# Two residual blocks with three expert mixtures: a new order of experts with 32-row steps, and another home for clearing and modulation

## The chip, the cores and the metric

The kernel is one program on one core of a Trainium2 chip, in fp32. The metric is the device time of one execution in microseconds (us). Its five engines are PE (matmul), DVE and ACT (elementwise), POOL (GpSimd; here also indirect DMA) and SP, which issues most DMA.

## The reference, cut to what matters

The input x has 512 tokens of 1024 values; the second block also has a context of 256 tokens.

```python
def first_block(...):     # x: 512 x 1024
    h = rms_norm(x, norm_mix)                  # one linear for three branches
    # RWKV branch + differential attention (subln on its heads), gated, w_out
    x = x + mixer(h)
    x = x + hierarchical_moe(rms_norm(x, norm_ffn), ...)          # f1
    x = x + gate(rms_norm(x, norm_ple) @ w_ple_gate) * (p @ w_ple_proj)

def second_block(...):
    for l in range(2):
        mod   = silu(c)     @ ada_w[l] + ada_b[l]    # 6 rows of 1024
        mod_c = silu(c_ctx) @ ada_w[l] + ada_b[l]
        # even (l = 0): attention + pooling; odd (l = 1): neighbourhood attention
        x = x + g1 * mixer(modulate(rmsnorm(x), sh1, sc1))
        x = x + g2 * hier_moe(modulate(rmsnorm(x), sh2, sc2))     # f2, f3
    return rmsnorm(x, final_g)

def hier_moe(h, ...):     # f2: 768 tokens (with the context), f3 and f1: 512
    # best of 4 groups, then the 2 best of its 8 experts per token
    yb = (silu(xb @ w1[e]) * (xb @ w3[e])) @ w2[e]     # 32 experts, 1024 -> 512 -> 1024
    return scatter_add(weights * yb)
```

## The kernel before

The phases follow one another, each in its own block on all engines: `n1` norm, `rp` features, `rr` `rwkv_prepare`, `rc` `rwkv_chunks`, `rs` scan, `rf` `rwkv_finish`, `l1` linear, `h1` heads, `a1` `difference_phase`, `sub` `subln_phase`, `ty` and `to` transposes, `l3`, `tm`, `l5`; the mixture f1 (`f1r` routing, `f1e` experts); `np` norm, `pq`, `lg` linear; `ne` norm, `le`, `he`, `ae`, `lf`; f2; `no` norm, `lo`, `lv`, `ao`, `lr`; f3; `nf` norm. A phase begins when all engines have ended the one before.

**Experts.** `experts_phase` (L2301) takes 32 steps, one expert each. Every expert has 6 pieces of weights of 1 MB, which SP streams into a ring of SBUF slots of that size (19 in f1, 18 in f2 and f3): the first ones (`FIRST`: 17, 14, 15) are asked for at the start of routing, the other 2, 4 and 3 slots exist only in the experts phase (`grow`, L2271), and each later piece waits until PE has used the piece in its slot (`used`). In f2 and f3 the first three experts are fixed (29, 30, 31), so that their weights can be loaded before the routing is known; the others are ranked by load in the routing. `Plan` (L85) gives each step its width: 64 rows, 128 in the wide steps (6, 10, 18, 22, 26 in f2; 9, 19, 24 in f3), and a huge one (14) of two columns of 128 and 64 rows with the same weights. The n_wide most loaded ranks go to huge and wide steps, the rest in order of load to the others. f1 takes its experts in their own order at 64 rows. Tokens beyond a step's rows go to overflow passes of 128 rows (up to `MAXOV` = 19), written out behind the steps and run only if there are any. POOL gathers each step's token rows from `hbuf` (L2285) and scatters its results to `ybuf` (L2374). In a step of 64 rows PE puts the two halves of the output columns on partitions 0 to 63 and 64 to 127, DVE evicts y in one copy from 128 partitions (L2568), and the scatter sends 128 half rows of 2 KB. `Combine` later gathers each token's two rows from `ybuf`, weighs and adds them in the following norm phase (`np`, `no`, `nf`).

**Routing.** `route_phase` (L1811) norms the tokens, loads the router weights with two strided DMAs straight into `wr` (L1888, L1889: packets of 4 and of 32 values), then biases and table, and behind them the first weight pieces (L2279), all on SP.

**Modulation.** `mod` is computed beside other phases by `ModulationSide` in groups (layer, third): 8 pieces of 1 MB each, 4 matmuls of 2 rows per piece (L2802), a bias matmul (L2806), two strips of 512 columns copied by ACT (L2782) and two scaled by DVE, or all four by ACT, then a store to `modD`. `begin` loads a ring of pieces, the biases and the gain rows; `rest` loads the others as slots come free; `finish` stores. PE's first matmul waits for biases and gains together. `steps` tells how many pieces PE takes between the turns of a norm or heads phase. Homes: (0,0) and (0,1) in l1 and h1, (0,2) in np, (1,0) in ne, (1,1) in he and ae, (1,2) in no.

**Clearing.** `Clear` (L2812 on) zeroes a tile in `rr` and writes it over `ybuf`, 13 blocks of 2 MB, and a padded bias table (`relpad`), all from SP in `rc` (L2835, L2838); `clear.end` waits in l1.

## Time and profile before

| | us |
|---|---|
| median of 3 runs (lowest, highest) | 3363.59 (3363.01, 3367.09) |
| the profiled execution | 3371.78 |
| its span (mean granted clock 0.907) | 3370.0 |
| PE busy | 2734.9 (81%) |
| DVE busy | 1038.0 (31%) |
| ACT busy | 735.1 (22%) |
| POOL busy | 398.2 (12%) |
| HBM read, written | 784.29 MB, 67.08 MB |

The busy shares are means over stages of different kinds. The three mixtures lie at about 724 to 1260 (f1), 1762 to 2331 (f2) and 2795 to 3332 (f3); the rest is norms, linears, attention and the RWKV scan. A row of a window view reads: stretch, its length, busy us of PE, PE's weight loads, DVE, ACT and POOL with their numbers of instructions, the clock granted to PE as a share of 2.4 GHz, the mean busy share of the 16 DMA engines, and what they moved in GB/s. A timeline row reads: start, duration, engine, line, operation, tiles, and in brackets the idle time before it with what ended it.

### The profile page before, as it was taken

The numbers are of one execution on the slowest core, as the hardware profiler recorded it, in microseconds if no ns is written. First come the engines' busy times: TensorE is split into PE (matmuls) and PEld (weight loads), VectorE is DVE, ScalarE is ACT, GpSimd is POOL, SyncE is SP. The second block draws the span as 40 slices with busy tenths as digits, with TensorE's granted clock in tenths as the row PEclk, the third lists the DMA queues.
The fourth block names the chain that finished last, engine by engine and source line by source line (L and its number), as shares of the span: only waits on it lengthen the run. The fifth ranks groups of instructions, "written<-read, shape, count | busy, mean of one in ns | idle before, by whom it ended". The sixth has DMA issues, their size and how long they took to land. (4 is left out here: it accounts for less than half of the span.)

```text
span 3370.0 us, 42335 instructions
## 1 busy us (share of the span) xinstructions
PE 2734.9 (81%) x16276; PEld 1612.7 (48%) x16276; DVE 1038.0 (31%) x2048; ACT 735.1 (22%) x1436; POOL 398.2 (12%) x510
## 2 busy tenths in 40 slices
PE   7866896779888875695976999995788985999994
PEld 5666772663333323483763433442576773333331
DVE  3524317541111113426535111112612644111113
ACT  3412234221000003213612000001311752000001
POOL 0122000001111111000100111112000510111111
PEclk9889998889999996897997999998799997999998
DMA  4090523159999986422028999998401128999996
GB/s 132 7 338 22 166 60 152 60 186 406 410 407 410 414 342 213 153 79 103 5 75 348 402 406 416 413 414 339 157 13 55 30 62 308 401 415 414 417 420 246
DMA packets 217304, 826.99 MB, mean 245 GB/s; under 512 B 59279, under 2 KB 84111, under 8 KB 137228
## 3 DMA queue, kind: packets, MB, share of 16 engines
q1 hardware_dynamic: 189868, 747.55, 56.9%
q0 software_dynamic: 27232, 76.68, 6.2%
q8 instruction: 134, 2.20, 0.3%
q14 instruction: 70, 0.57, 0.0%
HBM read 784.29 MB, written 67.08 MB: 253 GB/s over the span
## 5 line engine op out<-in xcount | busy, mean ns | idle before, releaser
L2430 PE MATMUL f1e_psum_up<-f_raw,f1e_xT 128*64 128x512 f32 x712 | 208.5, 648 | 46.9 <-DMA f_raw<-in_w_up_dram 39.1
L2430 PE MATMUL f3e_psum_up<-f_raw,f3e_xT 128*64 128x512 f32 x640 | 157.6, 615 | 13.6 <-DMA f_raw<-in_moe_w_dram 13.6
L254 PE MATMUL l_psum_acc<-l_w_hi,m_hT_hi 128*128 128x512 f32 x288 | 114.8, 399 | 30.4 <-DVE l_w_lo L248 30.4
L2430 PEld LDWEIGHTS f1e_psum_up<-f_raw,f1e_xT 128*64 128x64 f32 x712 | 60.3, 147 | 139.0 <-issue 136.3
L256 PE MATMUL l_psum_acc<-l_w_hi,m_hT_lo 128*128 128x512 f32 x288 | 113.9, 396 | 0.0
L255 PE MATMUL l_psum_acc<-l_w_lo,m_hT_hi 128*128 128x512 f32 x288 | 113.3, 393 | 0.0
L2285 POOL DMA_INDIRECT f_xin<-hbuf,g_src x98 | 94.1, 960 | 119.0 <-DVE g_src L2170 72.0
L2430 PE MATMUL f2e_psum_up<-f_raw,f2e_xT 128*64 128x512 f32 x432 | 101.0, 600 | 6.4 <-DMA f_raw<-in_moe_w_dram 6.4
L2519 ACT ACTIVATE f2e_xT<-f2e_psum_xT 128x512 f32<-128x512 f32 (+1 forms) x33 | 22.3, 675 | 363.8 <-PE f2e_psum_xT L2398 363.8
L2519 ACT ACTIVATE f3e_xT<-f3e_psum_xT 128x512 f32<-128x512 f32 (+1 forms) x33 | 21.4, 649 | 332.9 <-PE f3e_psum_xT L2398 332.9
L2430 PEld LDWEIGHTS f3e_psum_up<-f_raw,f3e_xT 128*64 128x64 f32 x640 | 45.9, 140 | 87.3 <-issue 84.9
L2577 DVE TENSOR_TENSOR f1e_h<-f1e_sig,f1e_psum_up 64x512 f32<-64x512 f32 x32 | 21.7, 679 | 210.1 <-ACT f1e_sig L2530 210.1
L2519 ACT ACTIVATE f1e_xT<-f1e_psum_xT 128x512 f32<-128x512 f32 x32 | 19.1, 597 | 307.3 <-PE f1e_psum_xT L2398 307.3
L248 DVE TENSOR_TENSOR l_w_lo<-l_raw,l_w_hi 128x512 fp32r<-128x512 f32 x70 | 48.2, 692 | 123.1 <-ACT l_w_hi L243 123.0
L254 PE MATMUL lo_psum_acc<-o_hT_hi,lo_w_hi 128*128 128x512 f32 (+1 forms) x192 | 71.5, 373 | 16.9 <-DVE lo_w_lo L248 8.8
L2374 POOL DMA_INDIRECT ybuf<-f1e_y,g_dst x32 | 32.5, 1015 | 426.7 <-PE f1e_psum_xT L2398 386.1
L2450 PE MATMUL f1e_psum_y<-f_raw,f1e_hT 128*64 128x512 f32 x344 | 80.7, 604 | 1.9 <-DMA f_raw<-in_w_down_dram 1.0
L2577 DVE TENSOR_TENSOR f3e_h<-f3e_sig,f3e_psum_up 64x512 f32<-64x512 f32 (+1 forms) x33 | 22.5, 681 | 190.2 <-ACT f3e_sig L2530 160.4
L2577 DVE TENSOR_TENSOR f2e_h<-f2e_sig,f2e_psum_up 64x512 f32<-64x512 f32 (+1 forms) x33 | 22.5, 681 | 188.2 <-ACT f2e_sig L2530 143.5
L2568 DVE COPY f2e_y<-f2e_psum_y 128x512 f32<-128x512 f32 (+1 forms) x33 | 26.0, 789 | 173.7 <-PE f2e_psum_y L2450 173.7
L2568 DVE COPY f3e_y<-f3e_psum_y 128x512 f32<-128x512 f32 (+1 forms) x33 | 25.0, 756 | 169.7 <-PE f3e_psum_y L2450 169.7
L254 PEld LDWEIGHTS l_psum_acc<-l_w_hi,m_hT_hi 128*128 128x128 f32 x288 | 55.0, 191 | 41.9 <-DVE l_w_lo L248 30.8
(884 smaller groups left out, 6058.1 us busy)
## 6 DMA issues: line engine op xcount, KB each, us to landing
f_raw<-in_moe_w_dram SPq DMA_DIRECT2D x209, 1024.0 KB, 27.9
c_y<-in_moe_w_dram SPq DMA_DIRECT2D x64, 1024.0 KB, 27.7
f_raw<-in_w_gate_dram SPq DMA_DIRECT2D x45, 1024.0 KB, 28.8
f_raw<-in_w_up_dram SPq DMA_DIRECT2D x44, 1024.0 KB, 29.3
f_raw<-in_w_down_dram SPq DMA_DIRECT2D x43, 1024.0 KB, 29.5
c_rows<-in_moe_w_dram SPq DMA_DIRECT2D x41, 1024.0 KB, 28.4
...
```

Of the source, the lines that this page charges most:

```text
L248: return v.tensor_tensor(dst, src, hi.bitcast(F32), ALU.subtract)
L254: pe.matmul(out, lh, rh, start=first, stop=False)
L255: pe.matmul(out, lh, rl, start=False, stop=False)
L256: return pe.matmul(out, ll, rh, start=False, stop=last)
L2285: pool.indirect_dma_start(out=self.xin[q % 2][0:rows, :], out_offset=None, in_=hbuf[0:n * P, :], in_offset=bass.IndirectOffsetOnAxis(ap=R. ...
L2374: pool.indirect_dma_start(out=yh, out_offset=place, in_=y[q % 2][:, 0:512], in_offset=None, bounds_check=2 * N * P - 1, oob_is_err=False). ...
L2430: mm = pe.matmul(out[lo:lo + HALF, :], x[:, kk * HALF:(kk + 1) * HALF], w[z][:, k * FF:(k + 1) * FF], start=(kk == 0), stop=(kk == KD - 1))
L2450: mm = pe.matmul(out, lhs, w[:, c:c + 512], start=(kk == 0), stop=(kk == KF - 1))
L2519: act.activation(xT[q % 2][:, 0:cols], px[:, 0:cols], ACT.Copy).then_inc(x_out, 1)
L2568: v.tensor_copy(y[q % 2][:, 0:cols], py[:, 0:cols]).then_inc(y_done, 1)
L2577: v.tensor_tensor(h[0:rows, :], sg[0:rows, :], pu[banks_of[q][-1]][0:rows, :], ALU.mult).then_inc(h_done, 1)
```

## The change

- `Plan` gets `slim_at`: steps of 32 rows (3 to 10 in f2, 3 to 14 in f3) for the least loaded ranks, right behind the three fixed experts. Wide steps move to 13, 17, 21, 25, 28 (huge 15) in f2 and to 17, 21, 25 (huge 19) in f3. In a slim step PE works on four strips of 32 columns: gate and up each as two strips of 256 output columns, y as four strips of 256.
- Each step scatters whole rows of `ybuf` from its own 32, 64 or 128 partitions; the eviction of y is split, DVE taking the lower 512 columns (`y_low`), ACT the upper (`y_high`). `MAXOV` goes from 19 to 23 and the blocks to clear from 13 to 14.
- The whole ring exists from the start of routing: the slots that were made late are lent to the routing for rows and tokens, and their pieces are asked for as the routing gives them back. The router weights come contiguous into `wgc` and `wec`, and POOL copies them into `wr`. PE's and DVE's waits for weights and biases part.
- Clearing: 6 blocks in `rr`, 3 in `rf`, 5 and `relpad` in `a1`; `clear.end` in l3.
- Modulation: (0,2) moves from np to `a1` (first 4 pieces) and `sub`; the first pieces of (1,0) are loaded in lg, the rest from POOL in ne, with a ring of 2 that (1,1) then takes over; the spacing changes in ne, he and no; gain rows are waited for by DVE alone, biases just ahead of their matmul.

```diff
-MAXOV = 19
+MAXOV = 23
 SLOTS = (NE + 1 + MAXOV) * P
 HALF = P // 2
+QUART = P // 4
...
+        self.slim_from = NE - len(fixed) - len(slim_at)
         self.n_pass = NE + 1 if self.sorted else NE
-        self.width = [P if s in wide_at or s == huge_at else HALF for s in range(NE)] + [HALF]
+        self.width = [P if s in wide_at or s == huge_at else QUART if s in slim_at else HALF for s in range(NE)] + [HALF]
...
+            elif step in self.slim_at:
+                out.append(slim)
+                slim += 1
...
-RANKED = {NTA: Plan(FIXED, (6, 10, 18, 22, 26), 14), NT: Plan(FIXED, (9, 19, 24), 14)}
+RANKED = {NTA: Plan(FIXED, (13, 17, 21, 25, 28), 15, (3, 4, 5, 6, 7, 8, 9, 10)),
+          NT: Plan(FIXED, (17, 21, 25), 19, (3, 4, 5, 6, 7, 8, 9, 10, 11, 12, 13, 14))}
...
-        if mix:
+        if mix or side and not whole:
             @block.gpsimd
             def _(pool):
-                mix.pool(pool)
+                if mix:
+                    mix.pool(pool)
+                if side and not whole:
+                    side.rest(pool)
...
+            clear.write(sp, 0, 6)
...
-            clear.write(sp)
...
+            clear.write(sp, 6, 9)
...
+        halves = [[h[:, i * D:(i + 1) * D] for i in range(2)] for h in stream.lend()]
+        tok = [h[:, :] for h in stream.xin] + halves.pop(0)
+        rows_home = [h for pair in halves for h in pair]
+        many = sum(1 if k[1] is None else 2 for k in kinds)
+        rows_home += [s.sb(f"row{i}", [P, D])[:, :] for i in range(len(rows_home), many)]
+        SC, SH = [], []
+        for k in kinds:
+            SC.append(rows_home.pop(0))
+            SH.append(rows_home.pop(0) if k[1] is not None else None)
+        own_hT = [h.rearrange("p (k t) -> p k t", t=P) for h in rows_home[:2]]
+        hT = own_hT + [s.sb(f"hT{i}", [P, KD, P])[:, :, :] for i in range(len(own_hT), 2)]
...
+            sp.dma_start(wgc[:, :, :], wg.rearrange("(p k) n -> p k n", p=P)).then_inc(wr_in, 16)
+            sp.dma_start(wec[:, :, :], we.rearrange("(p k) n -> p k n", p=P)).then_inc(wr_in, 16)
             sp.wait_ge(padded, 2)
-            sp.dma_start(wr[:, :, 0:NG], wg.rearrange("(p k) n -> p k n", p=P)).then_inc(wr_in, 16)
-            sp.dma_start(wr[:, :, 8:NL], we.rearrange("(p k) n -> p k n", p=P)).then_inc(wr_in, 16)
-            sp.dma_start(br[:, 0:NG], bc_row(bg, NG)).then_inc(wr_in, 16)
-            sp.dma_start(br[:, 8:NL], bc_row(be, NE)).then_inc(wr_in, 16)
+            sp.dma_start(br[:, 0:NG], bc_row(bg, NG)).then_inc(br_in, 16)
+            sp.dma_start(br[:, 8:NL], bc_row(be, NE)).then_inc(br_in, 16)
...
-            stream.first(sp)
+            stream.first(sp, 0, stream.n_first)
+
+            for t in range(2, min(n, TOKS)):
+                sp.wait_ge(stored[t], 16)
+                sp.wait_ge(t_done, 2 * t + 2)
+            stream.first(sp, stream.n_first, stream.n_first + 1)
+            sp.wait_ge(h_done, n)
+            sp.wait_ge(lt_done, n)
+            stream.first(sp, stream.n_first + 1, stream.ring)
 
         @block.gpsimd
         def _(pool):
+            pool.wait_ge(wr_in, 32)
+            pool.tensor_copy(wr[:, :, 0:NG], wgc[:, :, :]).then_inc(wr_done, 1)
+            pool.tensor_copy(wr[:, :, 8:NL], wec[:, :, :]).then_inc(wr_done, 1)
...
-                pool.wait_ge(y_done, q + 1)
-                column = plan.order[q][1]
-                place = bass.IndirectOffsetOnAxis(ap=R.dst[:, column:column + 1], axis=0)
-                if wide[q]:
-                    pool.indirect_dma_start(out=ybuf, out_offset=place, in_=y[q % 2][:, :], in_offset=None,
-                                            bounds_check=N * P - 1, oob_is_err=False).then_inc(y_out[q % 2], 16)
-                else:
-                    pool.indirect_dma_start(out=yh, out_offset=place, in_=y[q % 2][:, 0:512], in_offset=None,
-                                            bounds_check=2 * N * P - 1, oob_is_err=False).then_inc(y_out[q % 2], 16)
+                pool.wait_ge(y_low, q + 1)
+                pool.wait_ge(y_high, q + 1)
+                column, rows = plan.order[q][1], rows_of[q]
+                pool.indirect_dma_start(out=ybuf, out_offset=bass.IndirectOffsetOnAxis(ap=R.dst[0:rows, column:column + 1], axis=0),
+                                        in_=y[q % 2][0:rows, :], in_offset=None, bounds_check=N * P - 1, oob_is_err=False
+                                        ).then_inc(y_out[q % 2], 16)
...
+                if slim[q]:
+                    for k in range(KF):
+                        for b in range(2):
+                            r = slice(QUART * b, QUART * b + QUART)
+                            part = h[r, 0:FF // 2].rearrange("t (p k) -> t k p", k=KF)[:, k, :]
+                            mm = pe.matmul(ph[HALF * b:HALF * b + HALF, k * QUART:(k + 1) * QUART], part,
+                                           tab[r, C_IDENT + QUART * b:C_IDENT + QUART * b + QUART], start=True, stop=True)
+                    mm.then_inc(ht_done, 1)
+                    return
...
+                elif slim[q]:
+                    w = [stream.have(pe, q, 2 * half + z) for z in range(2)]
+                    out = pu[banks_of[q][0]]
+                    for k in ks:
+                        kk = 4 * half + k
+                        for z in range(2):
+                            for b in range(2):
+                                lo = HALF * (1 - z) + QUART * b
+                                c = k * FF + FF // 2 * b
+                                mm = pe.matmul(out[lo:lo + QUART, 0:FF // 2], x[:, kk * QUART:(kk + 1) * QUART], w[z][:, c:c + FF // 2],
+                                               start=(kk == 0), stop=(kk == KD - 1))
+                            if k == 3:
+                                mm.then_inc(used, 1)
...
+                        for g in range(4 if slim[q] else 0):
+                            c = k * D + D // 4 * g
+                            mm = pe.matmul(py[QUART * g:QUART * g + QUART, 0:D // 4], hT[:, kk * QUART:(kk + 1) * QUART],
+                                           w[:, c:c + D // 4], start=(kk == 0), stop=(kk == KF - 1))
...
+            def take_y(q):
+
+                act.wait_ge(used, stream.index[q, 5])
+                if q >= 2:
+                    act.wait_ge(y_out[q % 2], 16 * (q // 2))
+                if slim[q]:
+                    act.activation(y[q % 2][0:QUART, 512:768], py[2 * QUART:3 * QUART, 0:256], ACT.Copy)
+                    act.activation(y[q % 2][0:QUART, 768:D], py[3 * QUART:P, 0:256], ACT.Copy).then_inc(y_high, 1)
+                elif wide[q]:
+                    act.activation(y[q % 2][:, 512:D], py[:, 512:D], ACT.Copy).then_inc(y_high, 1)
+                else:
+                    act.activation(y[q % 2][0:HALF, 512:D], py[HALF:P, 0:512], ACT.Copy).then_inc(y_high, 1)
...
-                cols = D if wide[q] else D // 2
-                v.tensor_copy(y[q % 2][:, 0:cols], py[:, 0:cols]).then_inc(y_done, 1)
+                if slim[q]:
+                    v.tensor_copy(y[q % 2][0:QUART, 0:256], py[0:QUART, 0:256])
+                    v.tensor_copy(y[q % 2][0:QUART, 256:512], py[QUART:2 * QUART, 0:256]).then_inc(y_low, 1)
+                else:
+                    rows = rows_of[q]
+                    v.tensor_copy(y[q % 2][0:rows, 0:512], py[0:rows, 0:512]).then_inc(y_low, 1)
...
+            v.wait_ge(self.g_in, 16 * sum(len(x) for x in self.scaled))
...
-            pe.wait_ge(self.b_in, 64 * len(self.groups) + 16 * sum(len(x) for x in self.scaled))
...
+                pe.wait_ge(self.b_in, 64 * len(self.groups))
...
+            side.rest(sp)
...
+            side.scalar(act, 0)
...
+        third = modulation.side(m, [(0, 2)], 4, lent=True)
...
+            def between(sp):
+                side.finish(sp)
+                third.begin(sp)
+                clear.write(sp, 9, clear.blocks)
...
-        side = modulation.side(m, [(0, 2)], 3)
-
-        def fetches(sp):
-            early(sp)
-            side.begin(sp)
-        norm_phase(nc, "np", xs, tab, A["norm_ple"], hT=hT, ahead=fetches, mix=mix, side=side, steps=(2, 2, 2, 2))
+        norm_phase(nc, "np", xs, tab, A["norm_ple"], hT=hT, ahead=early, mix=mix)
+        home = Scope(nc, "nm", keep=True, side="right")
+        side = modulation.side(home, [(1, 0)], 2)
...
-            side = modulation.side(r, [(1, 0)], 3)
-
-            def fetches(sp):
-                side.begin(sp)
-                ahead.fetch(sp)
             norm_phase(nc, "ne", xs, tab, A["norm_mix_g_2"][0], hT=hT, mods=[mods[is_x(t)] for t in range(NTA)],
-                       ahead=fetches, side=side, steps=(1, 2, 2, 1, 1, 1))
+                       ahead=ahead.fetch, side=side, steps=(2, 2, 2, 1, 1))
...
-                       side=modulation.side(w, [(1, 2)], 3), steps=(2, 3, 3), whole=True)
+                       side=modulation.side(w, [(1, 2)], 3), steps=(0, 2, 2, 2, 1, 1), whole=True)
```

## Rows read from the trace of the kernel before

**Rows 1.** Page, part 2: DMA share and GB/s in 40 slices

```profile
...
DMA  4090523159999986422028999998401128999996
GB/s 132 7 338 22 166 60 152 60 186 406 410 407 410 414 342 213 153 79 103 5 75 348 402 406 416 413 414 339 157 13 55 30 62 308 401 415 414 417 420 246
...
```

**Rows 2.** Windows of the f2 stage: busy us per engine, granted clock, DMA share, GB/s

```profile
...
core 0: us, PE busy (x) PEld busy (x) DVE busy (x) ACT busy (x) POOL busy (x), PEclk, DMA share, GB/s
1800.00:1820.00 20.00, 7.52 (x31) 6.76 (x32) 14.85 (x65) 0.32 (x2) 0.00 (x0) 0.51 0.84 353
1820.00:1840.00 20.00, 11.75 (x50) 5.03 (x52) 6.17 (x26) 2.48 (x3) 2.89 (x3) 0.64 0.63 237
1880.00:1900.00 20.00, 20.00 (x101) 7.81 (x98) 2.49 (x4) 2.21 (x3) 3.21 (x4) 1.00 1.02 404
...
2280.00:2300.00 20.00, 15.36 (x68) 6.01 (x68) 2.10 (x4) 1.19 (x2) 1.97 (x2) 0.91 1.01 401
...
```

**Rows 3.** Windows of the f3 stage

```profile
...
2880.00:2900.00 20.00, 20.00 (x98) 7.54 (x96) 2.90 (x5) 1.78 (x3) 2.87 (x3) 1.00 1.02 388
3060.00:3080.00 20.00, 20.00 (x82) 8.35 (x82) 3.02 (x4) 1.19 (x2) 1.96 (x2) 1.00 1.01 423
3280.00:3300.00 20.00, 16.53 (x80) 6.72 (x82) 2.90 (x5) 1.72 (x3) 1.97 (x2) 1.00 1.02 425
...
```

**Rows 4.** Timeline of DVE: the h product of two half steps and the one behind a wide

```profile
...
1889.99 0.68 DVE L2577 TENSOR_TENSOR f2e_h<-f2e_sig,f2e_psum_up 64x512 f32<-64x512 f32 x1 [4.52 <-ACT f2e_sig L2530]
...
1902.30 0.68 DVE L2577 TENSOR_TENSOR f2e_h<-f2e_sig,f2e_psum_up 64x512 f32<-64x512 f32 x1 [4.59 <-ACT f2e_sig L2530]
...
1938.34 0.68 DVE L2577 TENSOR_TENSOR f2e_h<-f2e_sig,f2e_psum_up 64x512 f32<-64x512 f32 x1 [4.00 <-ACT f2e_sig L2530]
...
```

**Rows 5.** Timeline of SP: f2's first issues in the experts phase

```profile
...
1827.93 2.26 SPq L2346 DMA_DIRECT2D f2e_raw<-in_moe_w_dram  x4
1836.71 0.36 SPq L2346 DMA_DIRECT2D c_rows<-in_moe_w_dram  x1
...
```

**Rows 6.** Timeline of SP: the issue behind the router loads, f1 and f3

```profile
...
725.82 1.76 SPq L1890 DMA_DIRECT2D f1r_br<-in_b_group_dram  x1
...
2797.23 3.14 SPq L1890 DMA_DIRECT2D f3r_br<-in_moe_b_group_dram  x1
...
```

**Rows 7.** Window of f1, all steps of 64 rows

```profile
...
1000.00:1020.00 20.00, 17.10 (x74) 6.30 (x72) 1.79 (x3) 1.19 (x2) 1.96 (x2) 0.91 1.01 414
...
```

**Rows 8.** Waits in np and in ne: us in total, times, longest

```profile
...
PE np_psum_ada L2802 <- DMA pl_adag<-in_norm_ffn_g_dram: 33.0, 1, 33.0
ACT pl_hT_hi L243 <- PE np_psum_pt L430: 21.9, 5, 13.5
...
PE ne_psum_ada L2802 <- DMA e_adag<-in_norm_mix_g_dram: 25.5, 1, 25.5
...
```

**Rows 9.** Timeline of np, DVE: start, us, line, tiles

```profile
...
1285.28 1.28 DVE L2684 SCALAR_TENSOR_TENSOR np_first<-c_y,g_f1wts,np_first 128x1024 f32<-128x1024 f32 x1 [2.06 <-DMA c_y<-ybuf,g_f1slots]
...
1297.99 0.69 DVE L248 TENSOR_TENSOR pl_hT_lo<-np_psum_pt,pl_hT_hi 128x512 fp32r<-128x512 f32 x1 [8.71 <-ACT pl_hT_hi L243]
...
1316.25 1.29 DVE L248 TENSOR_TENSOR pl_hT_lo<-np_psum_pt,pl_hT_hi 128x512 fp32r<-128x512 f32 x2 [0.46 <-ACT pl_hT_hi L243]
...
```

**Rows 10.** Windows of rr (113), rf (319) and subln (596)

```profile
...
113.00:162.00 49.00, 35.18 (x168) 25.30 (x172) 36.10 (x47) 30.11 (x52) 16.81 (x12) 0.72 0.00 0
319.00:337.00 18.00, 0.00 (x0) 0.00 (x0) 16.88 (x30) 5.67 (x9) 0.00 (x0) 0.59 0.03 7
596.00:606.00 10.00, 0.00 (x0) 0.00 (x0) 9.43 (x7) 1.07 (x2) 0.00 (x0) 0.50 0.05 7
...
```

**Rows 11.** Window in which the clears are written now

```profile
...
180.00:250.00 70.00, 46.13 (x1268) 44.65 (x1268) 15.86 (x14) 10.15 (x17) 21.85 (x18) 0.89 1.03 377
...
```

**Rows 12.** Timeline of PE in np: the last pieces of the side

```profile
...
1309.75 1.89 PE L2802 MATMUL np_psum_ada<-pl_adaw,g_silu_c 128*2 128x512 f32 x8
...
1313.29 1.04 PE L2806 MATMUL np_psum_ada<-pl_adab,g_tab 1*2 1x512 f32 x8
...
```

More of the change, by code:

```diff
@@ L100, in ranks @@
     def ranks(self):
-        large, small, last = 1, self.n_wide, NE - len(self.fixed)
+        large, small, slim, last = 1, self.n_wide, self.slim_from, NE - len(self.fixed)
         out = list(range(last, NE))
@@ L327, in _ @@
                 ahead(sp)
-            if side:
-                if whole:
-                    side.begin(sp)
+            if side and whole:
+                side.begin(sp)
                 side.rest(sp)
-                if whole:
-                    side.finish(sp)
+                side.finish(sp)
             if out is not None:
@@ L2239, in __init__ @@
         self.row_slots, self.lent = by_end[:len(onward.row_tiles)], by_end[:len(lent)]
-        own = iter([s.sb(f"raw{i}", [P, self.COLS]) for i in range(first - len(lent))])
-        self.raw = [lent[self.lent.index(slot)] if slot in self.lent else next(own) for slot in range(first)]
-        self.raw_in = [s.sem(f"raw{i}") for i in range(first)]
+        own = iter([s.sb(f"raw{i}", [P, self.COLS]) for i in range(self.ring - len(lent))])
+        self.raw = [lent[self.lent.index(slot)] if slot in self.lent else next(own) for slot in range(self.ring)]
+        self.raw_in = [s.sem(f"raw{i}") for i in range(self.ring)]
         self.spare = [slot for slot in range(first) if slot not in self.lent][:self.PER]
@@ L2269, in __init__, with lend, first @@
         self.place = {piece: q for q, piece in enumerate(self.fetched)}
-    def grow(self, s):
-        more = range(self.n_first, self.ring)
-        self.raw += [s.sb(f"raw{i}", [P, self.COLS]) for i in more]
-        self.raw_in += [s.sem(f"raw{i}") for i in more]
-    def first(self, sp):
-        for q, (step, j) in enumerate(self.fetched[:self.n_first]):
+    def lend(self):
+        return [self.raw[slot] for slot in range(self.n_first, self.ring)]
+    def first(self, sp, a, b):
+        for q in range(a, b):
+            step, j = self.fetched[q]
             sp.dma_start(self.raw[q][:, :], self.src[j][self.plan.fixed[step]]).then_inc(self.raw_in[q], 16)
@@ L2308, in experts_phase @@
     N = plan.n_pass
-    wide = [plan.width[column] == P for step, column in plan.order]
+    rows_of = [plan.width[column] for step, column in plan.order]
+    wide = [rows == P for rows in rows_of]
+    slim = [rows == QUART for rows in rows_of]
     UP = 3
@@ L2336, in _ @@
         def _(sp):
-            for q in range(stream.n_first, len(stream.fetched)):
+            for q in range(stream.ring, len(stream.fetched)):
                 step, j = stream.fetched[q]
-                if q >= stream.ring:
-                    sp.wait_ge(used, stream.freed(q - stream.ring))
+                sp.wait_ge(used, stream.freed(q - stream.ring))
                 if step < len(plan.fixed):
@@ L3023, in first_mixer @@
                 linear(lhs, KD, allt, win[:, 3328:5376], 2048, gate_evac, on="a")],
-                early=side, late=clear.end)
+                early=side)
             qT, kT = q.sb("qT", [P, 4, SEQ]), q.sb("kT", [P, 4, SEQ])
@@ L3091, in ple @@
                                 linear(operand(pT), 2, allt, A["w_ple_proj"], D, add, behind=0)], ahead=ahead,
-                     late=side.finish)
+                     early=side)
+    return home, side
 def gated_add(rows_of, xs, G):
@@ L3129, in even_mixer @@
         pj = m.sb("pj", [P, NTA, 1280])
-        under = modulation.side(m, [(1, 1)], 2)
+        under = modulation.side(m, [(1, 1)], 2, lent=True)
+        under.W = side.W
         with Scope(nc, "e3") as r:
@@ L3302, in fused_blocks @@
         if stage("ple"):
-            ple(nc, tab, A, xq, modulation, behind)
+            home, side = ple(nc, tab, A, xq, modulation, behind)
         ctx = g.sb("ctx", [P, XT0, D])
```

176 lines of the change are left out of this document (95 added, 81 removed).

## The prediction

> **What bounds the kernel now.** I read the page's slices first [rows 1]. Three stretches of the span have the DMA share at 9 with 400 to 420 GB/s: the three mixtures of experts (f1, f2, f3), over half of the time. Elsewhere DMA is mostly idle and PE, or a chain of ACT and DVE, sets the pace. Then the windows by 20 us inside f2 and f3 [rows 2, 3]: share 1.00 to 1.02 from the start of the experts to a few us before their end, while PE has idle time in the last ones (15.36 of 20 at 2280, 16.53 at 3280). So the experts end when their last weight piece lands; 192 pieces of 1.05 MB have to come whatever the order of the experts. What moves an end there is bytes, bytes per second, or the moment the stream starts and stops. Last I read the phases around the moved modulation and clearing, by waits and timelines: np, subln, ne, the router heads.
>
> **The order of the experts: 0 in the middle, +1 at the end of f3.** PE's period is 12.25 us for a 64-row step (1889.99 to 1902.30) and 23.8 for a 128-row one (1902.30 to 1938.34 is one wide and one half) [rows 4]. The stream needs longer than a half step: 6 pieces are 6.29 MB, with the token rows about 6.7 MB, and at 408 GB/s 16.4 us. A 32-row step has no row; its ends are well under half of 12.25 and all of it. I take 7 us, nearest to a half step with its columns side by side, and it does not matter: anything below 16.4 waits for weights. What a slim step saves is idle time of PE. What the order does change is how far PE lags when the wide steps come late. In f3, from lag 0 at step 17: +7.6, −4, +20 (the expert run over two columns, taken as about 36 us), −4, +7.6, −12, +7.6, and six half steps at −4 each end near 0; the peak is 27 us. With 18 pieces of 2.6 us the ring holds 47, so the stream should go on, though with few requests in flight. For f2 the same sum peaks near 24 and ends at 0. I take +1 for f3, bounds 0 to +8 over both.
>
> **More pieces before the routing ends: 0.** In f2 DMA has 14 pieces done before the experts begin (share 0.84, then 0.63 in the next window) [rows 2], and 4 more are asked for at 1827.93, the first one into a freed slot at 1836.71 [rows 5]. After the change the 4 come early, in idle time, but the next must still wait for the first freed slot near 1837: 4 pieces (10 us) less to carry, 9 to 10 us of fresh idleness. Net −1 to +2.6; I take 0. In f1 and f3 DMA runs on from the first piece, so the order of issue buys nothing; the new waits on SP (stored tokens, h_done, lt_done) have only these pieces behind them.
>
> **Router weights: −2 in f1, −3 in f3, 0 in f2.** The 16-byte and 128-byte packets of the two router loads hold SP: the issue behind them takes 1.76 us in f1 and 3.14 in f3 [rows 6], where a plain issue takes 0.36 [rows 5]. Contiguous loads bring the first weight piece forward by 1.4 and 2.8, with a little for the cheaper issues themselves, one for one where DMA then never stops. f2 has slack before its experts. Two POOL copies and three small DVE operations of 0.15 to 0.2 us each in the order of ranks, with 23 rows for 19, lengthen routing by 0.3 to 0.6, which is +0.5 in f2. Bounds for the whole: −6 to +1.
>
> **Scatter of whole rows: 0, with a large upper bound.** A 64-row step used to send y from 128 partitions in halves; now 64 (or 32) partitions send whole rows of 4 KB. Bytes are equal. The gather already goes to 64 partitions in those steps, and there the stream is slower: 388 GB/s at 2880 with half steps of many tokens, against 423 at 3060 around a wide step and 425 at 3280 with small experts [rows 3]; f1, all in half steps, runs at 414 [rows 7]. 388 for 423 over 20 us is 1.6 us for some 100 gathered rows. The gathers alone explain it, if writing into few partitions crowds the weights, which are written too; the scatter reads. I take 0, as reads and writes are the nearest difference, and keep 16 us per thousand rows as the upper end. The eviction of y, now half on DVE and half on ACT, was one DVE copy of 0.69; its place behind the last weights stays about as long, and ACT's wait for y_out has slack: 0 ± 0.3 per stage.
> The Trainium skill, "SBUF — State Buffer", section "Door 1: The DMA port swizzle", says that partitions 0 to 63 reach only 8 of the 16 ports, and 0 to 31 the same 8. That agrees with the slower windows beside gathers; it does not say whether reads and writes meet at a port. By it alone the scatter would now be confined as the gather is, and the sum would be the third rival's.
>
> **Modulation (0,2) leaves np: −21.** In np PE waits 33.0 us for the gain rows that the side's first matmul wants, and ACT 21.9 for PE's transposes [rows 8]. DVE is idle for 8.71 us up to 1297.99, that is from 1289.3 on; its last operation is at 1316.25 to 1317.54 [rows 9]. Without the side the last combine (its data used at 1285.28) sets the end: it, the add, the square and the norm, each about 1.28 as that row (1285.3 to 1290.5), two turns on PE near 1.0 each, the high halves on ACT and the low ones on DVE at 0.69 each, and on DVE the backlog of earlier tiles at 1.4 each. That chain ends at 1295 to 1297. 1317.5 − 1296.3 = 21.2. Bounds −15 (the gathers, in POOL's queue, land no earlier and turns pile up) to −24 (they no longer share DMA with 3 MB).
>
> **It enters subln: +11.** Today 10.3 us of DVE alone, PE at 0 and clock 0.50 [rows 10]. Four of 8 pieces come in the difference phase behind nothing, but 5 clearing blocks are issued behind them: 4.2 + 10.5 MB at 377 GB/s [rows 11] are 39 us, the relpad rows some 9 more, from 551 to about 600. PE takes 1.9 us per piece at that clock [rows 12], frees the slots at 598 to 604, and the other four land 5 to 8 us after that, behind the rest of the clearing: 606 to 613. Then 1.9 for the last, 1.04 for the bias [rows 12], and about 1.4 each for ACT and DVE to take two strips of 512 columns each (at 0.69 each) [rows 9]: 617 against 606. Bounds +8 to +15. The difference phase ends with SP's last issue near 595, just where it ends now: +1 (0 to +3). finish in ty: +0.5.
>
> **Clearing in rr and rf: +1.** Six blocks of 2.1 MB (34 us) fall in 113 to 162, where DMA stands at 0.00, and three in 319 to 337 at 0.03 [rows 10]; the last lands near 338 to 341, just ahead of l1's first weights. rc gives up its writing, for which nothing waited.
>
> **(1,0) leaves ne's front, (1,1) and (1,2) re-spaced: −1.** In ne PE waits 25.5 us for the gain [rows 8] and ends the phase with side work; with two pieces in SBUF beforehand and the gain waited for only by DVE, it ends 2 us earlier (−5 to +2: a ring of 2 costs a landing per pair; POOL, which issues the rest, has nothing else there). In no, DVE paces: +1 (0 to +2). lg and he: 0, their PE works on loads that stay within 2 to 4 tenths of DMA [rows 1] and cover 2 to 4 MB more.
>
> **Sum.** −21 + 11 + 1 + 0.5 + 1 − 1 = −8.5; experts 1 + 0 − 5 + 0.5 = −3.5; together −12 of the profiled execution's 3371.8, of which 3370.0 is span: 3359.8. That execution is 8.2 above the median of the runs, 3363.6; carried over, 3351.6. I shade it to 3353 because edits costed at 0 seldom come below it.
>
> **Rivals.**
> 1. The stream gains too: PE catches up early, slots come free sooner, and the early windows of f2 and f3, now 404 and 388 [rows 2, 3], come up to f1's 414 or part of the way, 2 to 4% over 150 us each. For it: those windows have PE at 20.00. Against: DMA share is 1.01 there already. It would give 5 to 10 more: 3345.
> 2. np gives half (its turns and combine stay late) and subln costs +15, or the late wide steps run the ring dry for some us: −12 + 6 + 4 + 4, 3366, no change.
> 3. Slower: the scatter from 64 partitions crowds the weights as the gather does. 1024 rows of f1, about 1000 in f2's and 650 in f3's steps below 128, at 16 us per thousand, are 43 us at most; reads of the scatter may overlap half, so +15 to +43. It decides from 12 us on. At the middle, 3353 + 30: 3383. For it: only steps below 128 rows show slow windows. Against: that the windows show one direction's collision already paid.
> 4. The change doesn't do what it says: an expert overflows its 32 rows and passes over again. By the sorted loads of these inputs, from the reference, the slim ranks hold at most 29 tokens, so I give it next to nothing.
>
> **Chances.** Forecast 0.45, rival 1 0.12, rival 2 0.2, rival 3 0.21, rest 0.02. About 0.2% (6.7 us) is what a measurement of this kernel tells from no change: 3356.9 to 3370.3. The forecast's own range is 3346 to 3361, some of it inside that band. Faster 0.58, same 0.2, slower 0.22. The range for 8 in 10 runs from 3343 to 3386, to the middle of rival 3.
>
> **What would show it.** After: np without a side ends some 36 us after f1's last y, not 57; subln lasts 21 us with PE in it; first f1 piece issued 1.7 us after today's distance from the phase start; f2's DMA idle until its first freed slot; in f2 and f3 the h products of slim steps spaced 16 us, not 7. If windows of half steps in f1 fall below their 414 GB/s [rows 7] while the DMA share stays at 1.0, rival 3 is right; if they rise, rival 1. The forecast is wrong if the expert stages move by more than 5 us in all, or np and subln together by other than −10 ± 5.

## The result, and the profile after

The changed kernel took 3329.86 us in the median of 4 runs (3326.91 to 3337.80), the kernel before 3365.34 (4 runs, 3363.01 to 3377.89) on that occasion: ratio 0.9891, 95% interval 0.9861 to 0.9921. Measured a second time beside other kernels it was 3330.61 (ratio 0.9891, 0.9875 to 0.9908). The gain is about 36 us where I forecast 10, and the time lies below my range (3343). The direction was right; about three quarters of the gain came from a place to which I gave the price 0.

The profiled execution took 3337.80 us with a span of 3336.0, against 3371.78 and 3370.0. This table takes the length of a stage as the time from the last instruction of the stage before it to its own last one, in each kernel's profiled execution. "Clears moved" is the kernel before with that part of the change alone; the last column is the second profile of the changed kernel. The stages that are left out differ by 2 us at most.

| stage | before | clears moved | after | after, again |
|---|---|---|---|---|
| rr | 46.7 | 45.2 | 43.4 | 45.2 |
| rc (rwkv_chunks) | 114.2 | 87.9 | 87.4 | 87.9 |
| rs | 44.2 | 44.3 | 46.3 | 43.8 |
| l1, h1, a1 | 258.1 | 257.7 | 262.0 | 257.7 |
| sub | 10.6 | 10.6 | 22.9 | 21.3 |
| l5 | 47.9 | 49.1 | 49.0 | 49.1 |
| f1r + f1e | 541.0 | 540.4 | 538.2 | 537.6 |
| np | 53.8 | 52.5 | 33.3 | 33.2 |
| pq, lg | 66.0 | 65.7 | 66.2 | 65.0 |
| ne | 48.0 | 47.7 | 44.3 | 44.6 |
| f2r + f2e | 574.7 | 572.1 | 573.7 | 573.1 |
| f3r + f3e + nf | 572.1 | 574.7 | 572.9 | 571.8 |

What differs between the last two columns (rs, a1's group, rr) is what one profiled execution differs from another. What differs from the first in both is rc, sub, np, ne and f1.

**rc.** The windows of both kernels at the same times, inside rwkv_chunks: before, with the clears in it,

```profile
...
180.00:200.00 20.00, 13.64 (x405) 13.17 (x403) 4.88 (x4) 2.99 (x5) 6.82 (x6) 0.94 1.03 379
200.00:220.00 20.00, 13.38 (x382) 13.00 (x382) 3.82 (x4) 2.39 (x4) 4.99 (x4) 0.91 1.04 383
220.00:240.00 20.00, 12.46 (x344) 11.96 (x346) 5.18 (x6) 3.58 (x6) 7.49 (x6) 0.91 1.03 381
...
```

and after, without:

```profile
...
180.00:200.00 20.00, 18.40 (x617) 18.08 (x615) 7.32 (x6) 4.08 (x8) 8.74 (x8) 1.00 0.02 4
200.00:220.00 20.00, 16.10 (x485) 15.59 (x482) 7.26 (x7) 3.82 (x7) 8.49 (x7) 0.91 0.01 3
220.00:240.00 20.00, 18.41 (x617) 18.08 (x614) 7.37 (x7) 3.58 (x6) 7.62 (x6) 1.00 0.02 4
...
```

DMA share 1.03 to 1.04 against 0.01 to 0.02, and PE gets through 344 to 405 matmuls in 20 us against 485 to 617. The waits of the kernel before over this stage (engine, line, waited for: us in total, times, longest) name no DMA tile and no other engine for the difference, but "issue", which is idle time in which the engine waited for nothing that the profile shows:

```profile
...
PE ri_psum_p L1551 <- issue: 11.5, 4, 3.3
PE ri_psum_p L1560 <- issue: 10.2, 5, 3.6
...
PE ri_psum_p L1564 <- issue: 1.1, 1, 1.1
...
```

The first two lines are 21.7 us in 9 stops, all three 22.8 us in 10 stops of up to 3.6 us. After, the same view has no such line for a PE matmul; DVE's wait for PE (63.0 us before) is

```profile
...
DVE ri_x L1609 <- PE ri_psum_p L1571: 40.3, 16, 7.9
...
```

Behind "issue" stand PE's own instructions. The page counts instructions as DMA queues of their own; the one below has packets of 16 KB (2.20 MB in 134):

```profile
...
q8 instruction: 134, 2.20, 0.3%
...
```

In the records of that queue, before, the packets in this stage start at 184.7, 191.7, 198.9, 206.2, 213.5, 220.5 us and so on; after, at 182.8, 187.2, 191.3, 195.4, 199.8, 4.1 to 4.4 apart where PE runs through and 4.6 in the mean of the stage. The stage issues 2176 matmuls of 64 columns and as many weight loads and takes 17 of these packets, 256 such instructions for each, so that PE eats a packet in some 4 us; with busy DMA engines the next one came after 7.3 in the mean.

That this queue feeds PE shows in the stops: each of the 10 before ends 1.3 to 1.5 us after a packet of it has landed (the packet of 191.7 lands at 192.6, and PE goes on at 194.1; that of 206.2 at 207.2, and PE goes on at 208.7). Over the five kernels with traffic in rc, all 45 stops on "issue" end 1.2 to 1.6 us after a landing; the changed kernel and the one with the clears moved have none. A packet takes 0.9 to 1.4 us on its way with and without traffic, so it starts late; since when it was asked for, the trace doesn't say.

Not all of the difference is idle time. In the kernel with the clears moved rc is 26.3 us shorter: PE is idle for 21.1 us less (35.6 to 14.5) and busy for 5.2 us less (78.6 to 73.4) with the same 2176 matmuls. The granted clock hardly differs over the stage (0.89 before, 0.90).

**np and the issue order** went as forecast, **sub** by its length. In np no modulation is left; PE waits for DVE's norm, and DVE for the gathers:

```profile
...
PE np_psum_pt L435 <- DVE np_h L410: 28.3, 4, 22.7
...
DVE np_first L2759 <- DMA c_y<-ybuf,g_f1slots: 11.5, 3, 8.2
...
```

In sub PE takes the four pieces that were there, then waits 4.46 us for the fifth:

```profile
...
571.87 5.45 PE L2877 MATMUL sub_psum_ada<-m_adaw,g_silu_c 128*2 128x512 f32 x32 [0.71 <-PEq L207]
581.79 1.29 PE L2877 MATMUL sub_psum_ada<-m_adaw,g_silu_c 128*2 128x512 f32 x8 [4.46 <-DMA m_adaw<-in_ada_w_dram]
584.28 1.89 PE L2877 MATMUL sub_psum_ada<-m_adaw,g_silu_c 128*2 128x512 f32 x8 [1.20 <-DMA m_adaw<-in_ada_w_dram]
...
591.03 1.88 PE L2882 MATMUL sub_psum_ada<-m_adab,g_tab 1*2 1x512 f32 x8
...
```

SP shows when the missing pieces are asked for. It is held by the clears and relpad up to 570.1, and the refetches, whose turn comes in sub and behind its gain row, are issued at 574.86:

```profile
...
533.57 22.84 SPq L2912 DMA_DIRECT2D ybuf<-m_zeros  x5
556.45 13.66 SPq L2917 DMA_DIRECT2D relpad<-m_relrows  x2
...
574.86 3.50 SPq L2825 DMA_DIRECT2D m_adaw<-in_ada_w_dram  x4
...
```

The clears are the smaller part of that: with none of them in a1 (the last experiment) the refetches go out 2.0 us behind the gain row's issue instead of 3.0 and land in 7.6 us in the median instead of 9.0, but sub is still 19.9 us.

The issues that stood behind the strided router loads [rows 6] take 0.43 us now, in f1,

```profile
...
715.39 0.43 SPq L1906 DMA_DIRECT2D f1r_br<-in_b_group_dram  x1
...
716.81 0.43 SPq L2310 DMA_DIRECT2D f_raw<-in_w_gate_dram  x1
...
```

and in f3:

```profile
...
2761.97 0.43 SPq L1906 DMA_DIRECT2D f3r_br<-in_moe_b_group_dram  x1
...
2763.60 0.43 SPq L2310 DMA_DIRECT2D c_y<-in_moe_w_dram  x1
...
```

From the phase's first issue (714.07 in f1, 2760.18 in f3) to the first weight piece it is 2.7 us in f1 for 4.5 before, and 3.4 in f3 for 6.3.

**The experts.** Windows after; they answer to [rows 2, 3, 7]:

```profile
...
1000.00:1020.00 20.00, 16.73 (x76) 6.29 (x76) 2.47 (x5) 2.38 (x4) 1.85 (x2) 0.91 1.02 415
1200.00:1220.00 20.00, 18.25 (x83) 7.16 (x80) 2.47 (x4) 2.38 (x4) 1.86 (x2) 0.91 1.02 422
1784.00:1804.00 20.00, 11.31 (x50) 4.79 (x52) 5.19 (x20) 2.51 (x4) 2.82 (x3) 0.66 0.47 162
1840.00:1860.00 20.00, 17.11 (x267) 11.15 (x268) 3.59 (x10) 3.04 (x8) 3.61 (x4) 1.00 1.01 398
2845.00:2865.00 20.00, 17.70 (x189) 8.45 (x189) 3.32 (x7) 3.09 (x7) 3.69 (x4) 1.00 1.01 409
...
```

f1 runs at 415 and 422 GB/s with its scatter from 64 partitions, no slower than the 414 of before; DMA stands at 0.47 around the end of f2's routing, as predicted. The h products of the 32-row steps in f2 are 8.9 to 9.0 us apart while PE catches up and 16.8 once it has:

```profile
...
1839.82 0.41 DVE L2652 TENSOR_TENSOR f2e_h<-f2e_sig,f2e_psum_up 64x256 f32<-64x256 f32 x1 [4.03 <-ACT f2e_sig L2585]
...
1848.74 0.41 DVE L2652 TENSOR_TENSOR f2e_h<-f2e_sig,f2e_psum_up 64x256 f32<-64x256 f32 x1 [4.07 <-ACT f2e_sig L2585]
...
1866.69 0.41 DVE L2652 TENSOR_TENSOR f2e_h<-f2e_sig,f2e_psum_up 64x256 f32<-64x256 f32 x1 [4.12 <-ACT f2e_sig L2585]
...
1883.51 0.41 DVE L2652 TENSOR_TENSOR f2e_h<-f2e_sig,f2e_psum_up 64x256 f32<-64x256 f32 x1 [3.69 <-ACT f2e_sig L2585]
...
```

### The profile page after: what moved, and what is told of

It reads as the page before. It is cut to its first block and busy times, and to the rows that moved or that the text cites. A ratio compares the mean times of both kernels' runs of the same rounds, so it can differ in the third digit from the quotient of the medians.

```text
span 3336.0 us, 45180 instructions
## 1 busy us (share of the span) xinstructions
PE 2682.3 (80%) x17476; PEld 1626.9 (49%) x17476; DVE 1029.3 (31%) x2072; ACT 788.4 (24%) x1554; POOL 399.3 (12%) x526
## 5 line engine op out<-in xcount | busy, mean ns | idle before, releaser
L2479 PE MATMUL f3e_psum_up<-f_raw,f3e_xT 128*64 128x512 f32 x496 | 131.0, 618 | 13.3 <-DMA f_raw<-in_moe_w_dram 13.3
L2479 PE MATMUL f2e_psum_up<-f_raw,f2e_xT 128*64 128x512 f32 x480 | 114.8, 612 | 8.6 <-DMA f_raw<-in_moe_w_dram 8.6
L2468 PE MATMUL f3e_psum_up<-f_raw,f3e_xT 128*32 128x256 f32 x688 | 64.5, 496 | 31.7 <-DMA f_raw<-in_moe_w_dram 31.5
L2652 DVE TENSOR_TENSOR f1e_h<-f1e_sig,f1e_psum_up 64x512 f32<-64x512 f32 x32 | 21.7, 679 | 210.8 <-ACT f1e_sig L2585 210.8
L2400 POOL DMA_INDIRECT ybuf<-f2e_y,g_dst x33 | 30.7, 931 | 433.1 <-PE f2e_psum_xT L2425 352.8
L2598 ACT ACTIVATE f1e_y<-f1e_psum_y 64x512 f32<-64x512 f32 x32 | 19.0, 594 | 264.1 <-PE f1e_psum_y L2504 264.1
L2400 POOL DMA_INDIRECT ybuf<-f3e_y,g_dst x33 | 30.5, 923 | 420.7 <-PE f3e_psum_xT L2425 352.2
L2652 DVE TENSOR_TENSOR f2e_h<-f2e_sig,f2e_psum_up 64x512 f32<-64x512 f32 (+2 forms) x33 | 20.4, 617 | 188.2 <-ACT f2e_sig L2585 143.5
L2652 DVE TENSOR_TENSOR f3e_h<-f3e_sig,f3e_psum_up 64x512 f32<-64x512 f32 (+2 forms) x33 | 19.3, 584 | 189.7 <-ACT f3e_sig L2585 159.9
L247 ACT ACTIVATE l_w_hi<-l_raw 128x512 fp32r<-128x512 f32 x70 | 44.0, 631 | 122.2 <-PE l_psum_acc L260 108.4
L2455 PE MATMUL f2e_psum_up<-f_raw,f2e_xT 128*128 128x512 f32 x160 | 71.3, 599 | 0.0
```

The lines of the kernel that those rows point to most:

```text
L247: return act.activation(dst, src, ACT.Copy)
L2400: pool.indirect_dma_start(out=ybuf, out_offset=bass.IndirectOffsetOnAxis(ap=R.dst[0:rows, column:column + 1], axis=0), in_=y[q % 2][0:rows ...
L2455: mm = pe.matmul(out[:, :], x[:, kk * P:(kk + 1) * P], w[:, k * FF:(k + 1) * FF], start=(kk == 0), stop=(kk == KD - 1))
L2468: mm = pe.matmul(out[lo:lo + QUART, 0:FF // 2], x[:, kk * QUART:(kk + 1) * QUART], w[z][:, c:c + FF // 2], start=(kk == 0), stop=(kk == KD ...
L2479: mm = pe.matmul(out[lo:lo + HALF, :], x[:, kk * HALF:(kk + 1) * HALF], w[z][:, k * FF:(k + 1) * FF], start=(kk == 0), stop=(kk == KD - 1))
L2652: v.tensor_tensor(h[0:rows, 0:cols], sg[0:rows, 0:cols], pu[banks_of[q][-1]][0:rows, 0:cols], ALU.mult).then_inc(h_done, 1)
```

## The experiments

Each ratio is to the kernel before on the same chip.

### The clears moved, and nothing else

The kernel before with its 13 blocks in rr (6), rf (3) and a1 (4, with relpad).

```diff
+            clear.write(sp, 0, 6)        # rwkv_prepare
...
-            clear.write(sp)              # rwkv_chunks
...
+            clear.write(sp, 6, 9)        # rwkv_finish
...
+                clear.write(sp, 9, clear.blocks)   # a1, behind side.finish
```

> The kernel before with one part of the change: its 13 clearing blocks are written 6 in rr, 3 in rf, 4 and relpad in a1, none beside rwkv_chunks. Theory (the clears' traffic keeps PE waiting for its own instructions: PE shows 21.7 us of 'issue' idle in rc and its 16 KB instruction packets come every 7.2 us instead of 4.1): rc falls from 113 to 87 or 88 us, PE's issue idle there to under 2 us, the whole by 22 to 26 us: 3339 to 3343. Rival (rc is shorter for another reason, the granted clock or where tiles lie in SBUF with the new allocation): rc stays above 105 us and the whole within 5 us of the kernel before.

Measured: 3340.46 us (3340.05 to 3343.51), ratio 0.9914 (0.9893 to 0.9936): some 29 us faster (a little more than expected), rc 87.9. Its windows have the counts of the changed kernel (609, 435 and 617 in the second profile of it), not those of before:

```profile
...
180.00:200.00 20.00, 18.93 (x603) 18.71 (x602) 6.10 (x5) 4.18 (x7) 9.45 (x8) 0.94 0.02 4
200.00:220.00 20.00, 15.85 (x436) 15.50 (x433) 7.30 (x7) 4.18 (x7) 8.24 (x7) 0.83 0.01 3
220.00:240.00 20.00, 18.40 (x617) 18.08 (x613) 7.32 (x6) 4.02 (x7) 8.60 (x8) 1.00 0.02 4
...
```

This part alone gives 29 of the 36 us. The rival, clock or placement, is out: modulation, plan and tiles are those of before, and the granted clock over rc is 0.90 for 0.89.

### The clears back in rwkv_chunks

```diff
+        @block.sync
+        def _(sp):
+            clear.write(sp, 0, clear.blocks)     # rwkv_chunks; none in rr, rf, a1
```

> The kernel after with all 14 blocks and relpad written in rwkv_chunks again. Theory: rc back to 112 to 115 us with 20 us and more of issue idle of PE; sub gets shorter by 1 to 4 us as its last modulation pieces no longer stand behind clears; the whole +20 to +25: 3350 to 3355. Rival (rc's gain has another cause): rc stays near 88 us and the whole falls by the 1 to 4 us of sub.

Measured: 3358.70 us (9 runs, 3348.06 to 3360.89), ratio 0.9969 (0.9958 to 0.9980), 26 us above the changed kernel by the ratios, a little more than expected. The profiled execution is the fastest of the nine, 10.6 us below the median. In it rc is 116.5 us, sub 19.6 instead of 22.9, and PE's stops are back:

```profile
...
PE ri_psum_p L1567 <- issue: 9.3, 5, 3.6
...
PE ri_psum_p L1558 <- issue: 8.8, 4, 3.1
...
```

With 2.0 us on a third line that is 20.1 us in 10 stops. Of rc's 29 us more than in the changed kernel, 18 are idle time of PE; the other 11 are its busy time, 84.0 us for 72.9, at a granted clock of 0.83 over the stage for 0.91.

### One clearing block at a time

```diff
             sp.dma_start(dst, ...).then_inc(self.out, 16)
+            if i < self.blocks - 1:
+                sp.wait_ge(self.out, 16 * (i + 1))
```

> The kernel before, but in rwkv_chunks each clearing block of 2 MB is issued only when the one before has landed, instead of all queued at once (up to four outstanding, 19.2 us from issue to landing). If PE's 16 KB instruction packets wait behind everything that is queued (theory A, depth), one block outstanding lets them through in less: rc falls from 113 us to below 100 and the whole by 12 to 25 us. If they only get a share of busy DMA engines whatever stands behind (theory B, rate), the packets still come every 6.5 to 7.2 us while a block is under way; rc gains less than 8 us, by the gaps of about 2 us between blocks only.

Measured: 3384.22 us (3381.67 to 3388.30), ratio 1.0051 (1.0035 to 1.0068), slower by some 17 us where either theory had it faster. rc fell to 99.0 us, but SP was at the clears and relpad until 284 us, and the next stage waited 25.7 us for its turn. I had not seen that the wait between blocks stretches them past the end of rc. The windows:

```profile
...
180.00:200.00 20.00, 16.79 (x519) 16.47 (x517) 4.88 (x4) 4.23 (x8) 9.15 (x8) 0.93 0.68 250
200.00:220.00 20.00, 15.12 (x449) 14.48 (x446) 8.53 (x8) 2.51 (x5) 5.54 (x6) 0.92 0.62 228
...
```

```profile
...
PE ri_psum_p L1564 <- issue: 6.7, 3, 2.6
...
PE ri_psum_p L1560 <- issue: 2.2, 2, 1.8
...
```

"Issue" is down to 10.1 us in 7 stops. The packets came 3.5 to 8.4 us apart, 5.6 in the mean. Since DMA was busy only 62 to 70% of the time, this separates the two theories badly; hence the next one.

### Two blocks at a time

As above, but block i + 1 waits for block i − 1 (two semaphores in turn).

> The kernel before, with at most two clearing blocks (4 MB) outstanding in rwkv_chunks, so that DMA stays busy (share near 1.0, which one block at a time did not keep: 0.62 to 0.70) while little stands queued. If PE's instruction packets wait behind what is queued (depth), they come every 5.5 to 6.5 us and rc is 97 to 107 us. If the busy share alone sets it (rate), they come every 7 us and more, and rc is 110 us and more as in the kernel before.

Measured: 3367.06 us (10 runs, 3362.58 to 3369.03), ratio 0.9995 (0.9986 to 1.0005), rc 112.6 us.

```profile
...
180.00:200.00 20.00, 15.07 (x406) 14.61 (x404) 4.88 (x4) 2.55 (x5) 5.37 (x5) 0.83 1.03 378
...
220.00:240.00 20.00, 15.67 (x381) 15.40 (x381) 5.91 (x6) 3.58 (x6) 7.53 (x6) 0.74 1.03 378
...
```

```profile
...
PE ri_psum_p L1560 <- issue: 9.4, 4, 3.8
...
PE ri_psum_p L1551 <- issue: 6.8, 4, 3.0
...
```

4 MB outstanding, share 1.03, 18.4 us of "issue" in 9 stops, and the instruction packets are again 7.1 us apart. How much stands queued (19.2 us from issue to landing before, 11.3 here) makes next to no difference, 112.6 us for 114.2; whether the engines are busy all the time does.

### Reads instead of clears in rwkv_chunks

```diff
+            for i in range(28):      # 1 MB each, HBM to a spare tile
+                if i >= 2:
+                    sp.wait_ge(spare_in[i % 2], 16 * (i // 2))
+                sp.dma_start(spare[i % 2][:, :], ...).then_inc(spare_in[i % 2], 16)
+            for z in spare_in:
+                sp.wait_ge(z, 16 * 14)
```

> The kernel after with added traffic in rwkv_chunks: 28 pieces of 1 MB of expert weights read from HBM into two spare tiles, two outstanding, nothing waits for them but the end of the phase. It leaves out nothing. If any busy DMA starves PE of instructions (theory), rc grows from 87 to 105 to 116 us, with issue idle of PE of 10 us and more and instruction packets over 6 us apart: the whole +18 to +29. If it is the writing from SBUF to HBM alone that does it (rival), rc stays below 92 us.

Measured: 3351.01 us (3348.33 to 3354.79), ratio 0.9955 (0.9938 to 0.9971), 21 us above the changed kernel; but only 9.2 us of it is rc (96.6), another 12 is rs, whose start waited 12.2 us for the reads to end. In rc:

```profile
...
180.00:200.00 20.00, 16.71 (x473) 16.23 (x471) 4.88 (x4) 3.95 (x7) 7.91 (x7) 0.88 0.92 358
200.00:220.00 20.00, 14.55 (x455) 13.98 (x452) 8.53 (x8) 2.62 (x5) 5.97 (x5) 0.97 0.83 306
...
```

```profile
...
PE ri_psum_p L1580 <- issue: 3.5, 4, 1.6
...
```

Neither forecast was met: rc lies between them. Reads starve PE too (6.2 us of "issue" in 9 stops), so it is not the writing alone; at share 0.83 to 0.92 the packets come 5.3 us apart in the mean. Over the kernels that is 4.6 at a share of 0.02, 5.6 at 0.62 to 0.70, 5.3 at 0.83 to 0.92 and 7.1 to 7.3 at 1.03. This is no plain order by share, as the reads at the higher share did less harm than the single writes at the lower one. That gaps in the traffic let the packets through fits all four, but is not shown by itself, and whether reads at 1.03 would cost as much as writes wasn't tried.

### The order of before in f2 and f3

```diff
+RANKED = {NTA: Plan(FIXED, (6, 10, 18, 22, 26), 14), NT: Plan(FIXED, (9, 19, 24), 14)}
```

> The kernel after with the order and widths of before in f2 and f3 (no 32-row steps; wide 6, 10, 18, 22, 26 and 9, 19, 24, huge 14), all else as after. By my prediction the order is worth 0 (+1 in f3): within 3 us of the kernel after, f2 and f3 each within 2 us. Rival 1 (PE catching up early raises the rate of the stream, or the late wide steps change the end): f2 and f3 together 5 to 10 us longer than after.

Measured: 3335.30 us (3328.35 to 3338.34), ratio 0.9903 (0.9886 to 0.9921) against 0.9891 (0.9861 to 0.9921); that is 4 us, a little outside the 3 expected, with intervals that overlap. f2 is 572.9 us against 573.7 and 573.1 in the two profiles of the changed kernel, f3 with the final norm 572.1 against 572.9 and 571.8. The 32-row steps and the later wide ones, which gave the change its name, are worth nothing that can be told.

### Modulation (0,2) back in np

The changed kernel with that side in np (ring of 3, on SP) and none in sub.

```diff
+        gate_side = modulation.side(m, [(0, 2)], 3)
+        norm_phase(nc, "np", ..., side=gate_side, steps=(2, 2, 2, 2), rest_on="sp")
...
-            side.tensor(pe, 0, len(side.pieces))       # subln_phase
```

> The kernel after with modulation (0,2) back in np (ring of 3, on SP, 2 pieces ahead of each turn) and out of a1 and sub. By my steps of the prediction: sub back to about 10.5 us (-12), np longer by 15 to 21 us, net +3 to +9: 3333 to 3339. Rival (np's long end came mostly from the wait for the gain rows on PE, which the change takes off PE anyway): np only 3 to 10 us longer, net -9 to -2, so that the move itself bought nothing.

Measured: 3335.99 us (3331.26 to 3340.30), ratio 0.9906 (0.9883 to 0.9929), 5 us above the changed kernel by the ratios, though the intervals overlap. sub is 10.6 us again and np 47.7: 14.4 longer than after, 6.1 shorter than before. So of the 20.5 us that np gave, 14.4 come with the move, and sub takes back 12.3. The other 6.1 are at the most what it is worth that PE no longer waits for the gain rows: that was not tried alone, and np varies from 51.7 to 53.8 us over the profiles of the kernel before and its variants. PE in this np:

```profile
...
PE np_psum_ada L2879 <- DMA pl_adaw<-in_ada_w_dram: 33.6, 6, 28.6
ACT pl_hT_hi L247 <- PE np_psum_pt L437: 16.2, 4, 11.1
...
```

It now waits for the pieces themselves, 28.6 us at the longest for the 33.0 that it waited for the gain rows [rows 8].

### The last clears in l1's tail

The changed kernel with the 5 blocks and relpad of a1 behind l1's last weight piece.

```diff
+            if tail:
+                tail(sp)      # end of SP's loop in linear_phase l1: clear.write(sp, 9, clear.blocks)
```

> The kernel after with the 5 blocks and relpad of a1 written behind l1's last weight piece, where its DMA share is 0.00 for 20 us. Theory: the last four modulation pieces in sub land 5 to 8 us earlier, sub ends 4 to 7 us sooner; l1 or h1 may end 0 to 3 us later, since SP is held by the last issues; net -1 to -7: 3323 to 3329. Rival (sub is paced by PE at its low clock and not by the landings): sub as long as now, net 0 to +3.

Measured: 3343.34 us (3341.75 to 3350.24), ratio 0.9928 (0.9903 to 0.9953), 13 us slower than the changed kernel by the ratios. sub fell by 2.2 us, but h1 grew from 46.2 to 62.1. SP:

```profile
...
443.10 16.43 SPq L2914 DMA_DIRECT2D ybuf<-m_zeros  x5
459.57 14.87 SPq L2919 DMA_DIRECT2D relpad<-m_relrows  x2
475.17 3.81 SPq L663 DMA_DIRECT2D h_gain<-in_q_norm_dram  x1
...
```

relpad's issue holds SP until 474.4, and h1 finds its gain, rope and modulation loads behind 12 MB of clears: h_gain, 32 KB, takes 13.3 us from issue to landing. I had counted l1's quiet 20 us and not what h1 wants from DMA right after them.

### The last clears in l3's tail

The same `tail`, in l3, with `clear.end` in l5.

> The kernel after with the 5 blocks and relpad of a1 written behind the last weight piece of l3, where DMA is idle for 40 us of long matmuls, instead of in a1. sub falls from 22.9 to 19.6 to 20.7 us as in the two kernels without clears in a1, a1 by 0 to 1; tm and l5 start 0 to 2 us later. Net -1 to -4. If the clears hit h1-like fetches (as in l1's tail, +16 us), l5 would show it: its three first weight pieces landing after 665 and l5 more than 3 us longer.

Measured: 3328.01 us (3327.09 to 3330.11), ratio 0.9886 (0.9870 to 0.9903). It was then run again side by side with the changed kernel.

> The version with the last clears in l3, measured again on the same chip as the changed kernel. Its one execution had sub 3.1 us and a1's side 4.4 us shorter, of which only sub's 2 to 3 us are its own: 1 to 4 us below the changed kernel. If the difference is under 1 us, the clears in a1 cost nothing that can be told.

> The changed kernel itself, beside the next one on the same chip: ratio to before 0.989 as measured, 3326 to 3333 us.

Measured: 3330.46 (3323.59 to 3335.37), ratio 0.9885 (0.9867 to 0.9904), beside 3330.61 (3326.63 to 3334.32), ratio 0.9891 (0.9875 to 0.9908). sub is 19.8 and 19.9 us in the two profiles against 22.9 and 21.3, the fifth piece being waited for 1.81 us instead of 4.46:

```profile
...
572.04 5.13 PE L2879 MATMUL sub_psum_ada<-m_adaw,g_silu_c 128*2 128x512 f32 x32 [0.71 <-PEq L207]
578.97 1.04 PE L2879 MATMUL sub_psum_ada<-m_adaw,g_silu_c 128*2 128x512 f32 x8 [1.81 <-DMA m_adaw<-in_ada_w_dram]
...
588.99 1.03 PE L2884 MATMUL sub_psum_ada<-m_adab,g_tab 1*2 1x512 f32 x8
...
```

The 1.4 to 3.1 us in sub are there; in the whole they are below what the measurement tells. It is at best the equal of the changed kernel.

## Why the prediction was wrong

**The step that failed** is in "Clearing in rr and rf": "rc gives up its writing, for which nothing waited". I looked for a tile or an engine that waited for the clears and found none, priced the removal at 0, and gave no bound. It was −26.3 us, in a kernel where nothing else was changed, and +29 when put back (116.5 for 87.4). What waited was PE, for its own instructions, which come by DMA and came late beside the clears. The whole forecast of −12 with this term is −38, against −36 measured; that it fits so closely is in part luck, as ne, f1 and he were off by 1 to 2 us each and two profiles of one kernel differ by 11 us in all. The evidence was in the trace of before: 22.8 us of "issue" before PE's matmuls in rc, and a DMA share of 1.03 over the same stretch. The removed part deserved the same costing as the added ones: I counted what the clears would cost in their new homes (34 us of DMA in idle stretches) and not what their old home paid.

**np −21:** measured −20.5. The end that I built from the last gather (1296.3 for 1317.5) was right, but its cause was not fully understood: up to 6 us of it did not need the move.

**sub +11:** measured +12.3 and +10.7. The late refetches were rightly seen, but the clears in front of them are worth 1.4 to 3.1 us: without them sub is still 9.2 us longer than before. PE took 5.45 us for the first four pieces, not 7.6, and then waited.

**Clearing in its new homes, +1:** rr and rf cost nothing. The stretch from l1 to a1 was 257.7 for 258.1 with the clears moved and in the second profile of the changed kernel; the 262.0 of the first goes with matmuls in l1 233 ns apart for 229 and did not come back in the second.

**Router loads −2, −3:** the issues moved by 1.8 and 2.9 us. f1 gave 2.8 and 3.4, more than its spread: it takes 539.5 to 541.2 us in the four profiles with the routing of before and 536.9 to 538.6 in the nine with the new one. f3 with the final norm changed by +0.8 and −0.3, and over the same profiles it is 572.1 to 575.3 against 571.2 to 574.1, so that there a gain can't be told. If one is lost, what took it was not settled.

**Order and early pieces, 0 and +1:** for the order, by the old plan, +0.8 each with the first profile of the changed kernel and +0.2 and −0.3 with the second, so nothing. The early pieces were not tried alone. A 32-row step takes 9.0 us and not 7, without effect. (The 12.25 us of a 64-row step are 12.31 by the rows named.) Rival 1, a faster stream, did not occur: f2 and f3 gained nothing that can be told.

**Scatter, 0:** f1 has no 32-row step and no new order, but scatters from 64 partitions: 415 and 422 GB/s, and 538.2 us for 541.0. Rival 3, with up to 16 us in f1 alone, is out. The Trainium skill, "SBUF — State Buffer", section "Door 1: The DMA port swizzle", says that partitions 0 to 63 cover only 8 of the 16 ports; that a scatter which reads from them costs the weights anything does not show in f1.

**ne −2:** −3.7 and −3.4. **no +1, he 0:** −0.2 and +1.1. Rival 2 did not occur; rival 4 neither, as f2 and f3 did not grow.

**What stays open.** How full the DMA engines must be, and for how long without a gap, before instruction packets are late, and whether reads do as much harm as writes at the same share. What makes PE's busy time in rc 5 to 11 us longer with the clears in it, beside a lower granted clock in the second case. Why rr took 43.4 to 46.8 us in different profiles with the same work; in the two of the table the granted clock from 123 to 133 us was 0.67 (46.7 us) and 0.83 (43.4 us).
